# Gate and b projections of the mixing stages in pairs of weight blocks as seven quarter products, with the stages in another order

## The reference, cut to what matters

```
h = rmsnorm(x, norm_mix)
cb, cc, cu, q, k, v, g, ga, gb = split(h @ w_in)
z = causal_conv3(cc * cu)                        # per channel, 3 taps over the tokens
y_conv = (cb * z) @ w_conv_out
y_ret = (silu(g) * retention(q, k, v)) @ w_ret_out
merged = sigmoid(ga) * y_conv + sigmoid(gb) * y_ret
x = x + merged @ w_o
h2 = rmsnorm(x, norm_mlp)
x = x + square(relu(h2 @ w_up)) @ w_down         # 4096 wide
```

## Time and profile before

| | |
|---|---|
| median of 3 runs | 2442.28 us (2441.4 to 2442.53) |
| profiled execution, as a whole | 2441.91 us |
| its span (profiled instructions) | 2440.0 us |
| PE busy | 2427.2 us, 99% of the span |
| DVE, ACT, POOL busy | 1364.0, 952.1, 1373.5 us |
| CONV, RET and MIX, first layer | 167.65 to 472.65 us of the span |
| CONV from, second layer | about 1020.9 us |

### The profile page before, as it was taken

The page is one execution under the profiler, slowest core; times in us unless marked ns, Lnnn a source line. Parts: engine busy times, 40 slices in busy tenths (PEclk is TensorE's granted clock), DMA queues, the critical chain, the costliest instruction groups (busy, mean ns, idle before and its releaser), DMA issues.

```text
span 2440.0 us, 34632 instructions
## 1 busy us (share of the span) xinstructions
PE 2427.2 (99%) x12088; PEld 2020.4 (83%) x12088; DVE 1364.0 (56%) x1942; ACT 952.1 (39%) x1363; POOL 1373.5 (56%) x1682
## 2 busy tenths in 40 slices
PE   9999999999999999999999999999999999999999
PEld 7888888888998888888888889988777777888887
DVE  7884412358766768844123666538766665723333
ACT  5331232242543523312322424424577776422222
POOL 6556655556766755566555567657332334555554
PEclk9999999999999999999999999999999999999999
DMA  5222222242423422222222424353211112232322
GB/s 193 84 70 95 97 98 99 95 147 69 173 109 116 173 95 86 70 98 98 97 95 95 146 70 172 116 195 103 68 52 41 61 44 70 91 103 94 101 91 93
DMA packets 64912, 247.79 MB, mean 102 GB/s; under 512 B 7200, under 2 KB 9888, under 8 KB 63520
## 3 DMA queue, kind: packets, MB, share of 16 engines
q1 hardware_dynamic: 62496, 218.13, 26.6%
q10 hardware_dynamic: 2304, 28.17, 2.9%
HBM read 244.17 MB, written 2.10 MB: 101 GB/s over the span
## 4 chain that ended last, share of the span: by engine, by line
PE 92%; DVE 3%; ACT 2%; issue 1%; POOL 1%; DMA 0%; DVEq 0%; SPq 0%; ACTq 0%; POOLq 0%
PE ps L709 87%; PE ps L1092 1%; PE ps L1105 1%; PE ps L1121 1%; PE ps L1060 1%; POOL w_lo L606 1%; DMA w_raw<-weights 0%; ACT prob L1733 0%; PE ps L1125 0%; ACT set_hi L1420 0%; PE ps L784 0%; PE ps L900 0%; DVE sq_q L2550 0%; PE ps L1075 0%; POOL set_lo L627 0%
## 5 line engine op out<-in xcount | busy, mean ns | idle before, releaser
L606 POOL TENSOR_TENSOR w_lo<-w_raw,w_hi 128x256 fp32r<-128x256 f32 x1448 | 1191.8, 856 | 865.2 <-ACT w_hi L1341 644.1
L709 PE MATMUL ps<-H_hi,w_hi 128*128 128x512 f32 x1616 | 641.8, 397 | 0.2 <-DVE H_lo L2501 0.2
L709 PE MATMUL ps<-H_hi,w_lo 128*128 128x512 f32 x1616 | 629.5, 390 | 0.0
L709 PE MATMUL ps<-H_lo,w_hi 128*128 128x512 f32 x1616 | 629.2, 389 | 0.0
L1341 ACT ACTIVATE w_hi<-w_raw 128x1024 fp32r<-128x1024 f32 x295 | 310.1, 1054 | 482.4 <-PE ps L709 481.9
L709 PEld LDWEIGHTS ps<-H_hi,w_hi 128*128 128x128 f32 x1616 | 303.5, 188 | 69.3 <-issue 9.1
L709 PEld LDWEIGHTS ps<-H_lo,w_hi 128*128 128x128 f32 x1616 | 303.7, 188 | 65.0 <-issue 4.5
L709 PEld LDWEIGHTS ps<-H_hi,w_lo 128*128 128x128 f32 x1616 | 303.4, 188 | 63.7
L709 PE MATMUL ps<-A_lo,w_hi 128*128 128x512 f32 x744 | 289.6, 389 | 0.0
L709 PE MATMUL ps<-A_hi,w_hi 128*128 128x512 f32 x688 | 268.4, 390 | 0.0
L709 PE MATMUL ps<-A_hi,w_lo 128*128 128x512 f32 x688 | 267.8, 389 | 0.0
(11 more groups left out here) (331 smaller groups left out, 4027.1 us busy)
## 6 DMA issues: line engine op xcount, KB each, us to landing
w_raw<-weights SPq DMA_DIRECT2D x403, 512.0 KB, 3.3
mod_w<-mod_weights ACTq DMA_DIRECT2D x8, 3072.0 KB, 10.8
toeplitz<-biases SPq DMA_DIRECT2D x14, 128.0 KB, 2.1
out<-X SPq DMA_DIRECT2D x7, 256.0 KB, 2.0
X<-x SPq DMA_DIRECT2D x3, 512.0 KB, 7.8
decay_sb<-decay ACTq DMA_DIRECT2D x1, 1024.0 KB, 6.2
ctx_sb<-context ACTq DMA_DIRECT2D x1, 1024.0 KB, 13.8
X<-x SPq DMA_DIRECT2D x2, 256.0 KB, 4.0
```

Source lines behind the costliest of these rows:

```text
L606: last = nc.gpsimd.tensor_tensor(lo[:, c:c + LOW_COLS], w_raw[:, q, c:c + LOW_COLS], hi[:, c:c + LOW_COLS].bitcast(F32), ALU.subtract)
L709: mm = nc.tensor.matmul(dst, w[l], xs[r], start=start and a == 0, stop=stop and a == 2, skip_group_check=joined)
```

## The change

The b blocks, gate_b and gate_a of both hybrid layers are taken as pairs, in the way described for the feed-forward groups. To make whole runs of pairs the stages are put in another order: CU (16 jobs, c and u in turn), one run of eight pairs (four of b, four of gate_b; "the B run"), RET (8 jobs of ret-out alone), one run of four pairs (gate_a; "the GA run"), MIX (8 jobs of conv-out alone), O. A second set of token sums (`M_hi`, `M_lo`, scaled with norm_mix instead of norm_mlp) is made from x during CU and put where v lay. z after its taps is kept in `Alf` until b comes; b·z is split by ACT (`bz_high`) and DVE (`bz_low`) during the GA run; the sigmoids stand in the runs (`sigmoid`). The weight stream is laid out in the new order. SP's loads and POOL's lows in the new runs are written out instead of looped.

```diff
+MIX_RUNS = {L * LAYER_JOBS + first: pairs for L in range(DEPTH) for first, pairs in ((JOB_B, DT), (JOB_GA, DT // 2))}
+RUNS = {**FF_RUNS, **MIX_RUNS}
...
+        T_SETS = ((M_hi, M_lo, M_lo_f, PAR_NORM1), (T_hi, T_lo, T_lo_f, PAR_NORM2))
...
+            for n0, pairs in sorted(RUNS.items()):
+                start = n0 // RING + 1
                 if start > done:
...
+                for n in range(start * RING, start * RING + 2 * pairs):
                     load(n)
...
+                hi, lo = T_SETS[n in FF_STEP][:2]
+                T = lambda t: lambda k: (hi[:, t, k, :], lo[:, t, k, :])
...
+            def fast_run(n0, pairs, reduced=0):
+                for j in range(pairs):
+                    m = n0 + 2 * j
+                    last = j == pairs - 1
+                    fast_pair(m, 1)
+                    if j == 1 and reduced:
...
+                    fast_pair(m, 7)
+                    if j:
+                        fast_pair(m - 2, 4)
+                    fast_pair(m, 6)
+                    if j:
+                        fast_pair(m - 2, 3)
+                    fast_pair(m, 5 if last else 2)
+                    fast_pair(m, 2 if last else 5)
+                fast_pair(n0 + 2 * pairs - 2, 4)
...
-                jobs(n + JOB_CONV, CONV_JOBS, H_hi, H_lo, tiles + TILE_H)
-                with pe.Fori(0, PAIR_JOBS // RING) as i:
-                    for q in range(RING):
...
+                jobs(n + JOB_CU, CU_JOBS, H_hi, H_lo, tiles + TILE_H)
+                pe.wait_ge(t_ready, 4 * (2 * L + 1))
+                fast_run(n + JOB_B, DT)
+                jobs_behind(n + JOB_RET, C_hi, C_lo, tiles + TILE_OG)
+                fast_run(n + JOB_GA, DT // 2)
+                jobs_behind(n + JOB_MIX, C_hi, A_lo, tiles + TILE_BZ)
+                jobs(n + JOB_O, O_JOBS, A_hi, C_lo, tiles + TILE_MIX)
...
+            def first_pieces(n0, m):
+                for piece in (("A11", "S3"), ("S2", "S4"), ("A12",))[m]:
+                    piece_highs(piece, n0)
+                if m == 2:
+                    piece_highs("S1", n0)
+                    piece_highs("A22", n0)
...
+            def mix_run(n0, pairs, gates_from, tiles, bz):
...
+                for j in range(pairs):
+                    n = n0 + 2 * j
+                    more = j + 1 < pairs
+                    copy_first(n)
+                    if j:
+                        piece_highs("S1", n)
+                    if more:
+                        piece_highs("A11", n + 2)
+                    keep_third(n)
+                    if more:
+                        piece_highs("S3", n + 2)
+                    if j:
+                        piece_highs("A22", n)
+                    if not more:
+                        block_high(n0 + 2 * pairs, n)
+                    keep_second(n)
+                    if j:
+                        gate(n - 2, 1)
+                    if more:
+                        piece_highs("S2", n + 2)
+                        piece_highs("S4", n + 2)
+                    if j:
+                        gate(n - 2, 0)
+                    if bz:
+                        for m in range(j, j + 1 if more else DT):
+                            bz_high(m)
+                    if more:
+                        piece_highs("A12", n + 2)
+                last = n0 + 2 * pairs - 2
+                block_high(n0 + 2 * pairs + 1)
+                gate(last, 1)
+                gate(last, 0)
+                block_high(n0 + 2 * pairs + 2)
...
+                n = L * LAYER_JOBS
+                for a in range(CU_JOBS):
+                    if a + RING - 1 < CU_JOBS:
+                        ahead_at(n + JOB_CU + a + RING - 1)
+                    else:
+                        first_pieces(n + JOB_B, a + RING - 1 - CU_JOBS)
+                    if a == 1:
...
+                mix_run(n + JOB_B, DT, DT // 2, Af, False)
...
+                    else:
+                        first_pieces(n + JOB_GA, m + RING - 1 - DT)
+                mix_run(n + JOB_GA, DT // 2, 0, Clf, True)
+                for m in range(DT):
...
-                with dve.Fori(0, DT // RING) as i:
...
-                        fence()
-                        V.tensor_scalar(Af[:, 4, :], z[:, t % 2, 2:S + 2], column(PAR_CONV + 2 * DT, L, m), None, ALU.mult)
...
-                        fence()
...
-                        job_done(rs(s + 2), (s + 2) % RING)
-                        V.tensor_tensor(Blf[:, m, :], Af[:, 4, :], ps[:, (s + 2) % RING, :],
-                                        ALU.mult).then_inc(bank_free, 1)
-                        split(Blf[:, m, :], B_hi[:, m, :], B_lo[:, m, :])
...
-                        split(Alf[:, m, :], A_hi[:, m, :], A_lo[:, m, :])
...
+                def mix_run(n0, pairs, second, first, beside):
+                    for j in range(pairs):
+                        n = n0 + 2 * j
+                        more = j + 1 < pairs
+                        if j:
+                            add_c22(n - 2)
+                            sum_of("S1", n)
+                        if more:
+                            sum_of("S3", n + 2)
+                        if j:
+                            second_sum(n - 2)
+                            second(n - 2)
+                        if more:
+                            sum_low("S3", n + 2)
+                            sum_of("S2", n + 2)
+                            sum_low("S2", n + 2)
+                            sum_of("S4", n + 2)
+                        if j:
+                            first(n - 2)
+                        beside(j)
+                        if more:
+                            sum_low("S4", n + 2)
+                    last = n0 + 2 * pairs - 2
+                    fence()
+                    add_c22(last)
+                    second_sum(last)
+                    second(last)
+                    first(last)
...
+                def bz_low(m):
+                    dve.wait_ge(bz_high_ready, L * DT + m + 1)
+                    V.tensor_tensor(A_lo[:, m, :], Alf[:, m, :], C_hi[:, m, :].bitcast(F32),
+                                    ALU.subtract).then_inc(tiles_ready, 1)
+                def bz_lows(j):
+                    for m in range(j, j + 1 if j + 1 < DT // 2 else DT):
+                        bz_low(m)
...
+                for m in range(DT):
...
+                    V.tensor_tensor(Af[:, 3, :], ps[:, q, :], rstd_sq[:, :], ALU.mult).then_inc(bank_free, 1)
+                    fence()
+                    if m == 6:
+                        sum_of("S3", ahead)
+                    job_done(rs, q + 1)
+                    V.tensor_tensor(z[:, m % 2, 2:S + 2], Af[:, 3, :], ps[:, q + 1, :], ALU.mult).then_inc(bank_free, 1)
...
+                        sum_of("S2", ahead)
+                        sum_of("S4", ahead)
+                    V.tensor_scalar(Af[:, 4, :], z[:, m % 2, 2:S + 2], column(PAR_CONV + 2 * DT, L, m), None, ALU.mult)
...
+                    V.tensor_tensor(Alf[:, m, :], Af[:, 4, :], rstd[:, :], ALU.mult)
+                    if m in (1, 2, 3):
...
+                        sum_of("S1", ahead)
+                        sum_low("S1", ahead)
+                mix_run(n + JOB_B, DT, b_and_gate_second, b_and_gate_first, lambda j: None)
...
+                for m in range(DT):
+                    dve.wait_ge(ev_ready, L * EV_LAYER + EV_RET + 2 * (m // 2) + 2)
+                    job_done(r + (JOB_RET + m) // RING, m % RING)
+                    V.tensor_tensor(Af[:, m, :], Af[:, m, :], ps[:, m % RING, :], ALU.mult).then_inc(bank_free, 1)
+                    first_pair(n + JOB_GA, m)
+                mix_run(n + JOB_GA, DT // 2, lambda n: gate_second(Clf[:, 2 * STEP_OF[n] + 1, :]),
+                        lambda n: gate_first(Clf[:, 2 * STEP_OF[n], :], first_bank(n)), bz_lows)
```

More of the change, by code:

```diff
@@ L558, in _ @@
             done = 1
-            for L, g in FAST:
-                start = (L * LAYER_JOBS + JOB_FF + g * FF_GROUP_JOBS) // RING + 1
+            for n0, pairs in sorted(RUNS.items()):
+                start = n0 // RING + 1
                 if start > done:
                     load_rounds(done, start)
-                for n in range(start * RING, start * RING + DT):
+                for n in range(start * RING, start * RING + 2 * pairs):
                     load(n)
-                done = start + DT // RING
+                done = start + 2 * pairs // RING
             load_rounds(done, ATT_ROUND)
@@ L658, in _ @@
                             piece_lows("S1", m)
-                        if j + 1 < DT // 2:
+                        if j + 1 < pairs:
                             piece_lows("A11", m + 2)
@@ new lines, in t_sums @@
+                def t_sums(which, t):
+                    whole, base = T_SETS[which][2:]
+                    dve.wait_ge(diff_scaled, 2 * (2 * L + which) + (1 if t == T3 else 2))
+                    fence()
+                    half = slice(0, HALF_T) if t == T4 else slice(HALF_T, S)
+                    for k in range(HALF_K):
```

(38 more changed lines are left out.)

363 lines of the change are left out of this document (168 added, 195 removed).

## The result

The changed kernel takes 2448.54 us (median of 7 runs, 2447.87 to 2452.02) against 2442.53 for the kernel before (7 runs): a ratio of 1.0026 (95% interval 1.0016 to 1.0036), 6.0 us more. Forecast were 2440.2 us, within 0.2% of no change, with a range of 2433 to 2447. The time lies 1.5 us above the range.

The account below looks back on a forecast made before the run. PE, busy 99% of the span, was taken to bound the kernel. Net gains of 1.60 us (B run) and -0.55 (GA run) gave 1.05 per layer, 2.1 in both: 2440.2 us, range 2433 to 2447.

Parts of the forecast that it names:

- the granted clock stays full: PE across the trace: longest wait 1.2 us, clock full, so the sum put nothing for a slower clock.
- rival 3: B run start: PE idles about 3.3 us, clock falls to 1.2 GHz, 14.4 us in two layers, 2454.6; chance 0.08.
- a PEclk below 9 behind the start: Sign of a wrong forecast: the profile's granted-clock figure for PE falls under 9 behind the B run's start.
- gain of 24 pairs: PE: twelve pairs per layer replace 24 jobs, saving 9.60 us, 6.40 in the B run and 3.20 in GA.
- B run, start, the wait alone: B run's first S2 waits behind z and taps on DVE: 2.98 us per layer, besides an ordinary start loss of 0.40.
- B run, turn with the table load: ACT's first sigmoid needs a 1.28 us table load, making one B run pair late by 0.67 us per layer.
- B run, other turns: Starts of B run pairs behind another: five turns at 0.15 us each, 0.75 us per layer.
- GA run, start: GA run's first pair, behind the ret-out jobs: 0.40 us lost per layer, as in a feed-forward group.
- GA run, the turn behind step 0: GA run: bz_high and bz_low in step 0 delay pair 0's second; 0.80 us per layer, bounds 0.4 and 1.1.
- GA run, end, the wait alone: GA run's last S4 waits for add_c22 behind five bz_low: 2.4 us per layer, between 1.5 and 3.3.
- Nothing for CU, RET, MIX and O: Helper work in these stages stays covered by PE's matmuls; costed at nothing, idle PE there would prove it wrong.
- Rival 2: Turns of pairs: DVE meets POOL, 0.9 us in eight turns per layer, two layers lose 12 us, 2452.2; chance 0.09.

Follow-up runs that it names:

- e1: Changed kernel with the S3 quarter of the B run's first pair done three times, to keep PE at work in the wait: 2447.30 us, ratio 1.0015.
- e3: Changed kernel with the five bz_low of the GA run's last step put behind add_c22 instead of ahead of it: 2441.14 us, ratio 0.9993.
- e2: Changed kernel with the B run's first S1 sum ahead of the last CU job's z, its taps in steps 1 and 2: 2439.89 us, ratio 0.9987.
- e6: Changed kernel with e2, e3 and sigmoid table loaded in CU, plus the second block taken out of a turn's chain: 2428.45 us, ratio 0.9943.

## Why the prediction was wrong

The step that failed is the clock behind a wait, which the sum put at nothing: "the granted clock stays full" was read from a trace whose longest wait was 1.2 us and carried over to waits of some 3 us, each costed at its own length. The fall of the clock stood apart as rival 3, for the start of the B run alone, with a chance of 0.08 and a price of 14.4 us; a PEclk below 9 behind the start was named as a sign of being wrong, and it came. In the profile the clock fell behind both starts of the B run, 1.5 us each and 3.0 of those 14.4, since it lasted some 3 us and not five quarters, and behind one of two GA ends, where no rival had it: 1.3 us, 4.3 in all. With it alone the forecast would have been 2444.5, inside the range and on the side that was measured. The other terms below are 3.5 us over their forecast; the two together give 2448.0, and neither alone leaves the range. e1 shows that the idle time is the cause at the start; at the GA end e3 took the wait away, and the fall went with it.

The other terms, both layers together, in us, forecast and profile:

| term | forecast | measured |
|---|---|---|
| gain of 24 pairs | 19.2 | 19.2 |
| B run, start, the wait alone | 6.8 | 6.7 |
| B run, turn with the table load | 1.3 | 1.9 |
| B run, other turns | 1.5 | 1.9 |
| GA run, start | 0.8 | 1.0 |
| GA run, the turn behind step 0 | 1.6 | 1.8 |
| GA run, the other turn | 0.3 | 1.2 |
| GA run, end, the wait alone | 4.8 | 6.1 |
| clock behind the waits | 0 | 4.3 |

- **Start of the B run:** right in place, cause and length (e2 removes it by the order alone).
- **End of the GA run:** right in place and cause (e3), too small. I took the middle between 1.5 and 3.3 with "the cover half gone". The 3.3 is a slip: five subtractions of 0.96 from 728.2 and `add_c22`'s 0.41 end at 733.4, 3.0 behind 730.39. Of the five, two ran without POOL, as half a cover would have it, but the three beside it took 1.07 to 1.22 and not the 0.96 of the earlier trace rows; so the delay came out at that upper end.
- **Turns:** 6.8 us instead of 4.7. The largest miss is one GA turn of 1.0 us in the second layer, where an S3 sum on DVE waits 0.82 us for a weight load and then takes 1.22 us beside POOL; the profile of e2 has it too, those of e1 and e3 do not. In the B run of the first layer three `second` products took 1.28, 1.14 and 1.11 us, in the second layer 0.69 to 0.71 with the same order on POOL and DVE. The rows below this list show the first product of either layer: a product that starts just behind a subtraction of POOL's is long, and one that starts ahead of it is short while POOL's is long. What shifts the two engines against each other from one layer to the other is not settled here. That the product's place in the chain lets such a delay through is shown by e6 for the B run.
- **Table load:** 1.28 with nothing behind it, as taken, but the pair was 0.95 late and not 0.67. The load stood right behind `keep_second`, as forecast, but began 3.72 us ahead of the time at which the pair was due (316.15 against 319.87) where the sum had 3.91 (704.4 against 708.31), which is 0.19 of the miss; the other 0.10 is that a quarter's first matmul behind idle time takes 0.10 longer (its successor starts 0.22 us behind it instead of 0.12).
- **Nothing for CU, RET, MIX and O:** held; no wait of PE of 0.1 us or more was added in them.

```profile
273.21 0.75 POOL L640 TENSOR_TENSOR set_lo<-w_raw,set_hi 128x256 fp32r<-128x256 f32 x1
273.22 1.28 DVE L2353 TENSOR_TENSOR A_lo_f<-second_out,A_lo_f 128x512 f32<-128x512 f32 x1
...
1129.26 0.69 DVE L2353 TENSOR_TENSOR A_lo_f<-second_out,A_lo_f 128x512 f32<-128x512 f32 x1
1129.28 1.27 POOL L640 TENSOR_TENSOR set_lo<-w_raw,set_hi 128x256 fp32r<-128x256 f32 x1
```

Rival 2's mechanism, products and late loads that meet POOL at the turns, was there, but small: turns cost 6.8 us of the 24.8, 2.1 more than forecast and not 12.

## What to carry to other kernels

Where a bound engine gets less work, price each wait that the new order puts before it, and then ask what the wait does to the engine's clock: waits of about 3 us here cost half as much again (in nine of the ten such places in the profiles of the changed kernel and of e1 to e3). The first thing to read is the order on the helpers at a change of stage: an instruction that nobody is waiting for (taps, low parts of a later stage) standing ahead of one that PE waits for. Six such moves turned 6.0 us lost into 17.1 won with the same arithmetic.

## What the runs showed of the hardware

After 3.13 and 3.14 us without a matmul the granted clock was at half for some 3 us in both layers, at a cost of 1.5 us each. After 2.83 us it fell in the second layer (1.3 us, S4 and the first matmul of MIX) and not in the first, in the same execution and with the same order; in the profiles of e1 and e2 it fell behind this wait in both layers, so in five of six places. With 0.27 us of idle time at the place of the 3.14 it stayed full.

Where a 128x512 product of DVE and a 128x256 subtraction of POOL overlapped, the one that started first kept its length and the other was long: 1.28 us for DVE's when POOL's had started 0.01 us before it, 0.69 for DVE's and 1.27 for POOL's when POOL's started 0.02 us behind (otherwise they take 0.69 and 0.74).
